# Reordering the attentions of a transformer kernel: memory heads first, own heads last, with projections placed between the heads

## The reference, cut to what matters

```python
def first_block(x, mem, ...):
    mem_n = rmsnorm(mem, mem_norm_g)                       # 256 memory rows
    for i in range(2):
        hn = rmsnorm(x, attn_norm_g[i])
        if i == 0:   mix, q_cross = mla_mixer(hn, ...)     # 12 own heads, causal over all 512 keys
        else:        mix, q_cross = swa_mixer(hn, ...)     # 12 own heads, window of 128 keys, with sinks
        cross = memory_cross_attention(q_cross, mem_n, w_mem_kv[i])   # 4 heads over 256 memory keys
        x = x + concatenate([mix, cross]) @ w_o[i]         # the output projection
        x = x + squared_relu_mlp(rmsnorm(x, mlp_norm_g[i]), ...)
```

## Time and profile before

| | us |
|---|---|
| median of 3 runs | 1867.46 (1867.4 to 1867.64) |
| the profiled execution's own time | 1867.85 |
| its span | 1866.1 |
| PE busy | 1837.4 (98%) |
| POOL, DVE, ACT busy | 1049.2, 852.5, 769.4 |
| granted TensorE clock, mean | 1.000 |

### The profile page before, as it was taken

How to read it: one execution, slowest core, us unless ns; L and a number is a source line. 1 busy time by engine, 2 the same in 40 slices (tenths; PEclk the granted TensorE clock), 3 DMA queues, 4 the chain that set the end, 5 groups by cost and what they waited for, 6 DMA issues and landing times.

```text
span 1866.1 us, 26747 instructions
## 1 busy us (share of the span) xinstructions
PE 1837.4 (98%) x9071; PEld 1517.5 (81%) x9071; DVE 852.5 (46%) x1737; ACT 769.4 (41%) x1373; POOL 1049.2 (56%) x1436
## 2 busy tenths in 40 slices
PE   9999999999999999999999999999999999999999
PEld 6876788888888777888888888887778888888887
DVE  7786532222326674422222672797743354444200
ACT  6666542323233675423232353647643332233221
POOL 6862555555556864555555564555565556555553
PEclk9999999999999999999999999999999999999999
DMA  6330233232323212323323222221033223322332
GB/s 225 117 104 1 63 102 101 92 102 90 102 91 96 75 46 69 106 93 101 95 97 101 91 87 95 68 80 35 28 98 102 91 91 101 101 90 93 110 103 78
DMA packets 47582, 168.30 MB, mean 90 GB/s; under 512 B 5632, under 2 KB 5888, under 8 KB 47232
## 3 DMA queue, kind: packets, MB, share of 16 engines
q1 hardware_dynamic: 46512, 164.64, 27.4%
q10 hardware_dynamic: 976, 2.39, 0.5%
HBM read 164.13 MB, written 2.10 MB: 89 GB/s over the span
## 4 chain that ended last, share of the span: by engine, by line
PE 91%; POOL 3%; issue 3%; DVE 2%; ACT 1%; POOLq 0%; DVEq 0%; ACTq 0%
PE bank L714 27%; PE bank L716 27%; PE bank L715 27%; POOL WL L622 3%; PE bank L806 2%; PE bank L857 2%; PE bank L846 2%; PE bank L824 1%; PE bank L819 0%; ACT PROB L1187 0%; PE bank L757 0%; PE bank L996 0%; DVE PROB L1659 0%; PE bank L1041 0%; PE bank L1013 0%
## 5 line engine op out<-in xcount | busy, mean ns | idle before, releaser
L622 POOL TENSOR_TENSOR WL<-RAW,WH 128x256 fp32r<-128x256 f32 x1208 | 936.7, 806 | 683.6 <-ACT WH L1116 675.4
L714 PE MATMUL bank<-XH,WH 128*128 128x512 f32 x1311 | 520.3, 397 | 4.1 <-DVE KMV L1928 2.2
L716 PE MATMUL bank<-XH,WL 128*128 128x512 f32 x1311 | 510.8, 390 | 0.0
L715 PE MATMUL bank<-XL,WH 128*128 128x512 f32 x1311 | 510.6, 389 | 0.0
L1116 ACT ACTIVATE WH<-RAW 128x1024 fp32r<-128x1024 f32 x301 | 315.9, 1052 | 296.3 <-PE bank L716 293.7
L714 PEld LDWEIGHTS bank<-XH,WH 128*128 128x128 f32 x1311 | 246.2, 188 | 53.2 <-DVE KMV L1928 2.7
L716 PEld LDWEIGHTS bank<-XH,WL 128*128 128x128 f32 x1311 | 246.0, 188 | 52.1
L715 PEld LDWEIGHTS bank<-XL,WH 128*128 128x128 f32 x1311 | 246.5, 188 | 46.9
L714 PE MATMUL bank<-HH,WH 128*128 128x512 f32 x512 | 199.2, 389 | 0.0
L715 PE MATMUL bank<-HL,WH 128*128 128x512 f32 x512 | 199.2, 389 | 0.0
L716 PE MATMUL bank<-HH,WL 128*128 128x512 f32 x512 | 199.2, 389 | 0.0
(11 more groups left out here) (385 smaller groups left out, 2784.4 us busy)
## 6 DMA issues: line engine op xcount, KB each, us to landing
RAW<-stream SPq DMA_DIRECT2D x301, 512.0 KB, 3.4
out<-X SPq DMA_DIRECT2D x8, 256.0 KB, 4.6
X<-x SPq DMA_DIRECT2D x3, 512.0 KB, 8.0
MEM<-mem SPq DMA_DIRECT2D x1, 1024.0 KB, 10.4
W<-cmp_w ACTq DMA_DIRECT2D x1, 1024.0 KB, 4.6
KT<-KR ACTq DMA_DIRECT2D x1, 768.0 KB, 7.9
CT<-consts SPq DMA_DIRECT2D x1, 513.5 KB, 10.8
X<-x SPq DMA_DIRECT2D x2, 256.0 KB, 4.4
```

Source lines behind the costliest of these rows:

```text
L622: ins = pool.tensor_tensor(WL[:, slot, c], RAW[:, slot, c], WH[:, slot, c].bitcast(F32), ALU.subtract)
L714: pe.matmul(dst, lhs[0], rhs[0], start=start, stop=False)
L715: pe.matmul(dst, lhs[0], rhs[1], start=False, stop=False)
L716: return pe.matmul(dst, lhs[1], rhs[0], start=False, stop=stop)
```

## The change

In the first attention the 16 units of the memory heads come first and the 48 of the own heads last. Of the six outputs with the plain query channels only two are made before the attention (`EARLY_NOPE`). The other four, three products each, are made in bank 7 in TensorE's slots 1 to 3, 5 to 7, 9 to 11 and 13 to 15, and VectorE reads each out (two instructions) at the head of its slots 4, 8, 12 and 16; their scale row is first copied from ACC to RBC, since ACC is one of the rows of the attention. Bank 7 is taken from the transposes, which are left with two banks. The block order in output 0 of `wo0` starts with the memory heads, and seven of its eight products stand in slots 64, 64, 65, 66, 67, 68 and 69. ScalarE's high part of two weight tiles moves into slots 4 and 16, and GpSimd's low part of these two is cut in eight pieces between its scalings of own rows. In the second attention a query tile's products stand in slots 8t-17 to 8t-10, one to a slot (tile 2: two in slot 0, then slots 1 to 6), VectorE reads out in slot 8t-9, ScalarE splits in 8t-8 and makes the next weight tile's high part in 8t-18 (tile 2: slot 0). The six products of `wo1` move to slots 51, 55, 59, 64, 65 and 66.

```diff
+def is_cross(name, i):
+    return i < MH * NT if name == "mla" else name == "swa" and i >= NH * NT
...
-EARLY_Q, LATE_BANK, EARLY_K = 2, 7, 6
+EARLY_Q, LATE_BANK, EARLY_K = 2, 7, {"mla": 7, "swa": 6}
+EARLY_OUT = {"mla": (16, 16, 17, 18, 19, 20, 21), "swa": (3, 7, 11, 16, 17, 18)}
+EARLY_NOPE, NOPE_AT = 2, (1, 5, 9, 13)
+OUT_ORDER = {"mla": (6, 7, 0, 1, 2, 3, 4, 5), "swa": tuple(range(KD))}
...
         def mla_units():
-            return [Unit(...) for h, b in pair_order(NH)] + cross_units(0, lambda k: over_queries(MIX0, k))
+            return cross_units(0, lambda k: over_queries(MIX0, k)) + [Unit(...) for h, b in pair_order(NH)]
...
-        AFTER = {"mla": plan.out0["wo0"], ...
+        AFTER = {"mla": plan.out0["up0"] + FIRST_Q + NROPE + EARLY_NOPE, ...
-        TURNED = {name: [(o + 3) % RING, 4] + {"mla": [7], "swa": [], "nsa": [6]}[name] for name, o in AFTER.items()}
+        TURNED = {name: [(o + 3) % RING, 4] + {"mla": [], "swa": [], "nsa": [6]}[name] for name, o in AFTER.items()}
...
-            for n in range(late, converted("wo0")):
-                lo_part(n, n % RING)
+            lo_part(late, late % RING)
+            pieces = [(late + 1 + n // 4, n % 4) for n in range(8)]
             for i in range((NH + MH) * NT):
                 if normed_by_pool("mla", i):
                     normalise("mla", i)
+                    if not is_cross("mla", i) and pieces:
+                        n, piece = pieces.pop(0)
+                        lo_piece(n, n % RING, piece)
...
+            def late_nope(j):
+                def step():
+                    t, c, w, k, o, mark, start, stop = up0[late0 + j]
+                    if start:
+                        pe.wait_ge(drained, o)
+                    pe.wait_ge(lo_done, t + 1)
+                    ins = product(BANK[LATE_BANK][:], (WH[:, t % RING, c:c + w], WL[:, t % RING, c:c + w]),
+                                  (XH[:, KKV + k, :], XL[:, KKV + k, :]), start, stop)
+                    if mark:
+                        ins.then_inc(products_done, 1)
+                return step
...
+            late = {NOPE_AT[j // KQ] + j % KQ: [late_nope(j)] for j in range((NH // 2 - EARLY_NOPE) * KQ)}
+            for n, at in enumerate(EARLY_OUT["mla"]):
+                late.setdefault(NH * NT + at, []).append(early_output("mla", wo0, MIX0, n))
+            attention("mla", (signal("split_lo"), SPLIT_AT["mem"] + 2), meanwhile=late)
...
             for tile in range(EARLY_Q, 8):
                 for k in range(KD):
-                    slot = max(k - 3, 0) if tile == EARLY_Q else 8 * tile - 15 + min(k, KD - 2)
-                    late.setdefault(slot, []).append(late_query(tile, k))
-            for k in range(EARLY_K):
-                late[NH * NT + (1, 2, 4, 6, 8, 11)[k]] = [early_output(k)]
+                    late.setdefault(max(8 * tile - 17 + k, 0), []).append(late_query(tile, k))
+            late |= {NH * NT + at: [early_output("swa", wo1, Q1, n)] for n, at in enumerate(EARLY_OUT["swa"])}
...
-            keep_ahead(up0 + FIRST_Q + NROPE + NH // 2 - 1)
-            attention("mla")
+            nope = up0 + FIRST_Q + NROPE
+            keep_ahead(nope + EARLY_NOPE - 1)
+            attention("mla", {at + KQ: lambda o=nope + EARLY_NOPE + j: keep_ahead(o) for j, at in enumerate(NOPE_AT)})
...
-            late = {8 * tile - 7 - 2 * (tile == EARLY_Q): late_query(tile) for tile in range(EARLY_Q, 8)}
-            late |= {8 * tile - 14: lambda o=in1 + 6 + tile: keep_ahead(o) for tile in range(EARLY_Q, 8)}
+            late = {8 * tile - 8: late_query(tile) for tile in range(EARLY_Q, 8)}
+            late |= {max(8 * tile - 18, 0): lambda o=in1 + 6 + tile: keep_ahead(o) for tile in range(EARLY_Q, 8)}
...
-            for m in range(NH // 2):
-                both_halves(up0 + FIRST_Q + NROPE + m, QT0[0:HD, :, :], m, ACC)
+            def query_nope(m, scale=RBC):
+                both_halves(up0 + FIRST_Q + NROPE + m, QT0[0:HD, :, :], m, scale)
+            for m in range(EARLY_NOPE):
+                query_nope(m, ACC)
+            own.then(dve.tensor_copy(RBC[:], ACC[:]))
             dve.wait_ge(signal("late_consts_in"), 16)
-            attention("mla")
+            attention("mla", {at + KQ: lambda m=EARLY_NOPE + j: query_nope(m) for j, at in enumerate(NOPE_AT)})
...
-            late = {8 * tile - 8 - 2 * (tile == EARLY_Q): late_query(tile) for tile in range(EARLY_Q, 8)}
-            late |= {8 * tile - 5 - 2 * (tile == EARLY_Q): late_query_lo(tile) for tile in range(EARLY_Q, 8)}
+            late = {8 * tile - 9: late_query(tile) for tile in range(EARLY_Q, 8)}
+            late |= {8 * tile - 6: late_query_lo(tile) for tile in range(EARLY_Q, 8)}
```

More of the change, by code:

```diff
@@ L60 @@
 PAIRED = ("nsa",)
+def is_cross(name, i):
+    return i < MH * NT if name == "mla" else name == "swa" and i >= NH * NT
 def normed_by_pool(name, i):
     b = i % 8 // 2
[L65 removed]
+    return name == "nsa" or is_cross(name, i) or name == "mla" and b >= 2
 def copied_by_vector(name, i):
     b = i % 8 // 2
[L71 removed]
+    return b % 2 == 1 if is_cross(name, i) else name == "mla" and b == 3
 def count_before(of, name, i):
@@ L179, in make_plan @@
         mlp += shift(by_output(CH, KD), 16 * c, 16 * c) + shift(by_output(KD, CH), 16 * c + 8, 16 * c + 8)
-    p.stage("wo0", 8, 8, by_output(8, KD))
+    wo0 = by_output(8, KD)
+    p.stage("wo0", 8, 8, [wo0[m * KD + k] for m in range(8) for k in OUT_ORDER["mla"]])
     p.stage("mlp0", 64, 64, mlp)
@@ L532, in place_turned @@
                 b, odd, pair = i % 8 // 2, i % 2, i // 8
-                if i >= NH * NT:
+                if is_cross(name, i):
                     first = 2 * b
@@ L800, in attention @@
                                 pe.wait_ge(signal("gate_exp"), i + 1)
-                        if rotated and i < NH * NT and i % (4 * NT) == 0:
-                            pe.wait_ge(signal("q0_placed"), u.head // 4 + 1)
+                        if rotated and not is_cross(name, i):
+                            if i % (4 * NT) == 0:
+                                pe.wait_ge(signal("q0_placed"), u.head // 4 + 1)
+                            if i % (2 * NT) == 0 and u.head // 2 >= EARLY_NOPE:
+                                pe.wait_ge(drained, plan.out0["up0"] + FIRST_Q + NROPE + u.head // 2 + 1)
                         if name == "swa" and i % (2 * NT) == 0:
@@ L845, in attention @@
                         for kb in range(u.nb):
-                            ins = pe.transpose(BANK[TURNED[name][j % nt]][:, blk(kb)], row[:, blk(kb)], IDENT)
+                            ins = pe.transpose(BANK[TURNED[name][j % len(TURNED[name])]][:, blk(kb)], row[:, blk(kb)], IDENT)
                         ins.then_inc(signal(name + "_turned"), 1)
@@ L937, in _ @@
                   after={0: [scales("c_kv", column=RKV)], 1: [rotate_key], 4: [sums("c_q")], MEM1: [scales("c_q", column=RQ)]})
-            dense(lambda _: plan.steps["up0"], 0,
+            up0, late0 = plan.steps["up0"], len(plan.steps["up0"]) - (NH // 2 - EARLY_NOPE) * KQ
+            dense(lambda _: up0[:late0], 0,
                   lambda o, k: (XH[:, k if o < FIRST_Q else KKV + k, :], XL[:, k if o < FIRST_Q else KKV + k, :]),
@@ L942, in _, with early_output, step, late_first @@
                   ready=lambda o, k, i: (signal("c_lo"), (k if o < FIRST_Q else KKV + k) + 1, (k, o < FIRST_Q)))
-            attention("mla", (signal("split_lo"), SPLIT_AT["mem"] + 2))
-            dense(lambda _: plan.steps["wo0"], 0, lambda o, k: over_queries(MIX0, k), ready=heads_ready("mla"))
+            def late_nope(j):
[9 more added lines that the diff above has]
+                return step
+            def early_output(name, steps, own, n):
+                def step():
+                    t, c, w, k, o, _, start, _ = steps[n]
+                    if start:
+                        pe.wait_ge(drained, o)
+                        pe.wait_ge(lo_done, t + 1)
+                    pe.wait_ge(signal(name + "_lo"), n + 1)
+                    product(BANK[LATE_BANK][:], (WH[:, t % RING, c:c + w], WL[:, t % RING, c:c + w]),
+                            over_queries(own, k), start, False)
+                return step
+            def late_first(name, steps):
+                n = EARLY_K[name]
+                return steps[KD:KD + n] + steps[n:KD] + steps[KD + n:]
+            wo0 = plan.steps["wo0"]
+            late = {NOPE_AT[j // KQ] + j % KQ: [late_nope(j)] for j in range((NH // 2 - EARLY_NOPE) * KQ)}
+            for n, at in enumerate(EARLY_OUT["mla"]):
+                late.setdefault(NH * NT + at, []).append(early_output("mla", wo0, MIX0, n))
+            attention("mla", (signal("split_lo"), SPLIT_AT["mem"] + 2), meanwhile=late)
+            dense(lambda _: late_first("mla", wo0), 0, lambda o, k: over_queries(MIX0, k), ready=heads_ready("mla"),
+                  o0=plan.out0["wo0"], in_late_bank=plan.out0["wo0"])
             mlp("mlp0")
@@ L965, in _ @@
             wo1 = plan.steps["wo1"]
```

(13 more changed lines are left out.)

13 lines of the change are left out of this document (6 added, 7 removed).

## The result

The changed kernel takes **1875.38 us** (median of 6 runs, 1873.29 to 1876.04) against 1867.64 for the kernel before; the ratio is 1.0037, 95% interval 1.0027 to 1.0047. It is slower by 7.7 us where I forecast +3.2, inside my range. The profiled execution is the shortest one, 1873.29 us with a span of 1871.5: 5.4 us over the span before. So 5.4 us have to be found in this trace, and some 2 us in the other runs.

What follows compares the result with a forecast made beforehand. TensorE, busy for 98% of the span, was taken to bound the kernel. First attention +7.6 and second -4.4 gave +3.2 us: 1871.05 for the profiled execution, 1870.7 against the median, range 1863.5 to 1876.

Steps and rivals of the forecast that it cites:

- What bounds it: Whole kernel: TensorE is busy for 98% of the span, so time is won only where it idles; new waits cost in full.
- The start: First attention's start: TensorE idles 3.0 us, waiting for GpSimd's low memory keys and VectorE's read-out of the first two outputs.
- The three gaps: Between the four moved outputs in bank 7: products wait for VectorE's read-out, 1.9 + 1.85 + 1.85 = 5.6 us idle.
- the late exp table: First attention's start: ScalarE's late exp table load and ACC copy delay the first exponential; 0.6 us carried into the gaps, making 6.2.
- Slot 18: First attention: the fourth read-out delays VectorE's copy of unit 11, so transposes and values wait; 2.3 us idle.
- The lost bank: First attention's own pairs: with two transpose banks, values follow 0.35 us later in each of five pairs, 1.7 us.
- my rival on the lost bank: First attention: one more transpose held in each of six pairs adds 2.8 us, 1873.5; chance 0.36 together with half a second-attention win.
- What is won: First attention: idle time of the old start and end goes, 4.9 to 6.2 us, taken as 5.9.
- The second attention: Read-out waits go (-4.6), with start, `wo1` slot and end terms: -4.4 us in sum, bounds -2.5 and -6.
- The clock: Rival: clock falls to 1.2 GHz over the 12 products between the new gaps, 8.2 us more, 1878.7; chance 0.03.
- Gaps that close: Rival: VectorE's read-outs come in time, three gaps and slot 18 cost 0.5 us each, kernel at 1863.5; chance 0.14.
- The slower case: Rival: more transposes held by the lost bank, or only half the second attention's win, about 1873.5; chance 0.36.

Runs made afterwards that it cites:

- e6: The changed kernel with the four moved outputs started in slots 1, 8, 15 and 22 instead of 1, 5, 9 and 13: 1870.40 us, ratio 1.0014.
- e5: The kernel before with one edit, two banks instead of three for the first attention's transposes: 1870.74 us, ratio 1.0015.
- e4: The changed kernel with all six plain query outputs computed ahead of the first attention again: 1867.96 us, ratio 1.0002.
- e7: The kernel with only the second attention changed, plus VectorE's low split of a query tile in slot 8t-4 instead of 8t-6: 1864.36 us, ratio 0.9980.
- e9: The kernel with only the second attention changed, but its six `wo1` products back in slots 49, 50, 52, 54, 56 and 59: 1865.93 us, ratio 0.9989.
- e1: The changed kernel run once more without any edit, against the kernel before: 1874.82 us, ratio 1.0037.
- e8: The kernel before, old head order, with seven early `wo0` products inside the memory heads at the end, in the late bank: 1864.64 us, ratio 0.9982.
- e10: First attention of e8; second of e3 with VectorE's low split in slot 8t-4 except the first late tile, and seven early `wo1` products: 1857.83 us, ratio 0.9945.
- e3: The kernel before with only the second attention's part of the change: 1866.34 us, ratio 0.9993.
- e2: The kernel before with only the first attention's part of the change: 1875.66 us, ratio 1.0041.
- e12: As e10, with the first attention's pair read-outs on ScalarE and VectorE one slot later: 1855.68 us, ratio 0.9934.

## Why the prediction was right, and where it was wrong

**What bounds it** was right: busy time moved by 1.2 us, the rest of the 5.4 us is waits of TensorE.

**The start** (3.0 predicted) has two waits, for GpSimd's low keys and for the read-out, as the prediction named them: 1.42 + 1.24 = 2.7 us. (Such a figure begins only at the modelled end of the matmul before; by the starts TensorE stands for 3.0 us here and for 5.7 in the three gaps.) **The three gaps** (1.9, 1.85, 1.85) measured 1.97, 1.56 and 1.56, 5.1 us for 5.6; e6 shows that they are what I said, a chain of latency against one slot without a product. Of the 0.6 us for the late exp table, which I had added to them, at most 0.2 shows, a wait of VectorE for the exponential right ahead of the first read-out. **Slot 18** (2.3) was 1.2. **The lost bank** (1.7) costs 2.8 by e5: the mechanism and the period of 10.4 were right, but it also holds transposes at the start and in the memory heads, which is half of my rival on the lost bank (e5 has the old order; that the bank costs as much in the new one isn't shown). **What is won** (5.9) has no run of its own and is only a remainder: from 7.0 = 2.7 + 5.1 + 1.2 + 2.8 + 0.3 - x it is 5.1, or 4.3 if the own pairs' part of the bank (2.0) alone is counted. But the 5.9 took in idle time under modelled ends; with the waits counted so too (3.0 + 5.7, and 1.6 for slot 18) the remainder is 6.4 or 5.6, so this term isn't shown to be off. The sum, +7.0 for +7.6, is good partly because errors cancel: 1.1 us too little for the bank against 0.5 too much for the gaps with the exp table and 0.7 for slot 18. e4 splits it otherwise: 5.2 for the moved outputs, 1.8 for the order with its bank.

**The second attention** was the step that failed: 1.9 us won where I said 4.4. By its parts, with a product counted at 0.68 us: the start -0.3 (predicted -0.3: +1.5, +1.3, -3.1); the four own pairs -2.3 (predicted -3.8, four of the five waits); slots 47 to 54 +2.0 (predicted +0.7: +1.5 less the fifth wait of 0.8); the end -1.3 (predicted -1.0). So two terms were mis-sized, by 1.5 and 1.3 us:

- In the own pairs all waits for the read-out went, as I said, but with its steps one slot earlier and the weight tile's high part four slots earlier, VectorE's low split of a tile ran into GpSimd's low part of a weight tile, grew from 2 x 0.69 us to 0.80 + 1.11, and held the next unit's minimum, exponential and copy: 0.41 us a pair, 1.6 in all (how much of that is the slower split and how much its new slot, e7 leaves open). I had walked TensorE's slots and ScalarE's, and had taken VectorE's steps over at their old lengths. The Trainium skill ("SBUF — State Buffer", Who interferes with whom) states that a VectorE instruction with two SBUF inputs and a GpSimd instruction that reads SBUF block each other, the later one waiting in full. The trace agrees in kind: the second half, which began beside GpSimd's last piece, takes 1.11 us, and the half that the earlier trace rows shows 0.70.
- In slots 47 to 54 the chain sets the length, as I said, but I put the price at three quarters of the three products' 2.0 us; e9, where they come back and the stretch grows by 0.3, shows that it is nearly all of it (1.7).

**The clock** was the rival with the least chance and the wrong size. I let it fall to 1.2 GHz over the twelve moved products (8.2 us, 0.03) or not at all. It does fall behind the new waits, but in some executions only, and cost 3.1 us in e1's profile and nothing in the attentions of the first. This accounts for the 2 us by which the median lies above the profiled run as far as e1's profile can speak for the runs without one, and so for +5.4 in the trace having become +7.7 in the median. That one profile at full clock (1.00 in every stretch) says nothing of kernels with longer waits is the lesson of it.

**The other rivals.** Gaps that close did not happen. The slower case was given 0.36, with two mechanisms, a dearer bank and half a win in the second attention; both came in part, and the profiled run lies between it and the forecast. (Its extra hold, six times 0.49 us, is 2.9 us and not 2.8.)

**How much of it is luck.** The median lies 0.6 us under the top of my range, which I had put at most of the lost bank. The smaller win of the second attention explains the profiled run (+5.4 for +3.2); the last 2 us up to the median came from the clock, of which the range held nothing. By my own bounds (slower over 1871.2) the result is slower, to which I gave 0.42, and "same" had 0.45.

## What to carry to other kernels

Work moved into a loop of dependent slots needs its read-out done before the same bank is wanted again: count the slots between in latency, not in load, and give them (e6: seven slots apart instead of four took the gaps away). Before an order is turned round to fill its end, try to put the work into the old end (e8: -3.3 us, where the new order cost +1.8). When a step is moved, walk every engine that has a part in it, and look at what runs beside it on the others (e7). And add up a fix over the whole stage before it is given up: e9 won 1.75 us in slots 47 to 54 and lost 1.3 at the end, and e10, which filled the end as well, kept both.

## What the runs showed of the hardware

The granted clock fell to half behind waits of TensorE of 1.9 us at once (e1, e3, e7), of 4.6 us in three parts (e1) or of 2.7 us in two (e6), in some executions of a kernel and not in others. In e2's and e5's profiles it falls behind the wait of 1.45 us that the second attention of before has the earlier trace rows, where before's own profile shows 1.00. e7's profile has it in the 3 us behind a stretch with TensorE busy for 1.11 of 3.00 us:

```profile
697.00:700.00 3.00, 1.11 (x7) 0.96 (x7) 1.89 (x8) 2.94 (x9) 0.34 (x1) 0.95 0.00 0
700.00:703.00 3.00, 3.00 (x16) 3.00 (x15) 2.46 (x7) 2.12 (x9) 1.59 (x3) 0.50 0.00 0
```

The Trainium skill ("TensorE: Matmul & The Clock Gate", Part 1) states that idleness halves the array's clock and activity restores it; the trace agrees. What a fall costs differs: 1.55 us at each of the two places in e1; about 0.5 us in e2 and e5, where the start of the second attention takes 19.64 and 19.54 us against 19.10 before; nothing in e3. With the 1.9 us wait filled (e9, e10, e12) the profiles show no fall inside the attentions, and the runs of e10 lie within 1.1 us of each other and those of e12 within 0.9, against 2.5 for e1, though those of e9 still lie within 2.0. In a part of the executions, then, such waits of TensorE were paid more than in full.
